# One change to a transformer-block kernel: in the pass over peer_u, 64 of 256 tokens take their rows by indexed gathers

## What is computed

```python
def peer_ffn(h, wq, subkeys, u_tab, v_tab):
    q = (h @ wq).reshape(bsz, s, PEER_HEADS, 2, PEER_KEY_DIM // 2)
    s1 = jnp.einsum('bshd,kd->bshk', q[:, :, :, 0], subkeys[0]).astype(f32)
    s2 = jnp.einsum('bshd,kd->bshk', q[:, :, :, 1], subkeys[1]).astype(f32)
    v1, i1 = lax.top_k(s1, PEER_TOPK)
    v2, i2 = lax.top_k(s2, PEER_TOPK)
...
    best, pos = lax.top_k(cand, PEER_TOPK)
    eidx = jnp.take_along_axis(cidx, pos, axis=-1)
    gate = jax.nn.softmax(best, axis=-1).astype(h.dtype)
...
        act = jax.nn.gelu(jnp.einsum('td,tkd->tk', hx, u_tab[ex]))
        return jnp.einsum('tk,tkd->td', act * gx, v_tab[ex])
```

## Time and profile before

| what | value |
|---|---|
| runs | 3867.51, 3871.76, 3889.56 us |
| the profiled execution | 3888.6 us, span 3886.9 us |
| TensorE (PE) busy | 3543.7 us, 91% |
| VectorE (DVE) busy | 2507.0 us, 64% |
| ScalarE (ACT) busy | 1260.2 us, 32% |
| GpSimd (POOL) busy | 448.8 us, 12% |
| HBM | 753.14 MB read, 50.57 MB written, 207 GB/s |

### The profile page before, as it was taken

The page is one execution under the profiler, slowest core; times in us unless marked ns, Lnnn a source line. Parts: engine busy times, 40 slices in busy tenths (PEclk is TensorE's granted clock), DMA queues, the critical chain, the costliest instruction groups (busy, mean ns, idle before and its releaser), DMA issues. The chain is left out here.

```text
span 3886.9 us, 46926 instructions
## 1 busy us (share of the span) xinstructions
PE 3543.7 (91%) x19227; PEld 2825.6 (73%) x19227; DVE 2507.0 (64%) x3107; ACT 1260.2 (32%) x1433; POOL 448.8 (12%) x451
## 2 busy tenths in 40 slices
PE   7989878999999999999999799997987999899898
PEld 5756557799999999777777587486854766443576
DVE  6855777589777434778788645655446435695564
ACT  3323233334444433444444333223312101100333
POOL 0011110000110000772223000020000211000000
PEclk8888888999999999999999899998998999899899
DMA  9973476265876666999999553305643111553563
GB/s 357 381 237 123 124 279 241 104 218 188 302 263 244 232 227 223 340 357 379 369 365 386 190 185 123 92 6 168 220 167 109 33 44 55 147 152 125 180 237 141
DMA packets 300245, 807.48 MB, mean 208 GB/s; under 512 B 35120, under 2 KB 126356, under 8 KB 256256
## 3 DMA queue, kind: packets, MB, share of 16 engines
q1 hardware_dynamic: 269904, 674.83, 50.5%
q0 software_dynamic: 27664, 123.36, 8.3%
q10 hardware_dynamic: 2464, 6.29, 0.4%
HBM read 753.14 MB, written 50.57 MB: 207 GB/s over the span
## 5 line engine op out<-in xcount | busy, mean ns | idle before, releaser
L2453 DVE TENSOR_TENSOR expert_w_low<-expert_w,expert_w_high 128x2048 fp32r<-128x2048 f32 x256 | 585.7, 2288 | 334.5 <-ACT expert_w_high L2840 333.9
L2840 ACT ACTIVATE expert_w_high<-expert_w 128x2048 fp32r<-128x2048 f32 x256 | 489.5, 1912 | 321.2 <-DMA expert_w<-in_peer_v_dram 242.0
L2759 PE MATMUL bank<-h_high,expert_w_high 128*128 128x256 f32 x2048 | 583.0, 285 | 10.2 <-DVE expert_w_low L2453 9.2
L2760 PE MATMUL bank<-h_low,expert_w_high 128*128 128x256 f32 x2048 | 580.3, 283 | 0.0
L2761 PE MATMUL bank<-h_high,expert_w_low 128*128 128x256 f32 x2048 | 580.3, 283 | 0.0
L289 DVE TENSOR_TENSOR weights_low<-weights,weights_high 128x1024 fp32r<-128x1024 f32 (+4 forms) x288 | 338.2, 1177 | 328.6 <-ACT weights_high L272 325.4
L272 ACT ACTIVATE weights_high<-weights 128x1024 fp32r<-128x1024 f32 (+4 forms) x288 | 293.7, 1021 | 478.5 <-PE bank L317 391.9
L2759 PEld LDWEIGHTS bank<-h_high,expert_w_high 128*128 128x128 f32 x2048 | 393.9, 192 | 11.3 <-DVE expert_w_low L2453 10.0
L2760 PEld LDWEIGHTS bank<-h_low,expert_w_high 128*128 128x128 f32 x2048 | 394.0, 192 | 0.0
L2761 PEld LDWEIGHTS bank<-h_high,expert_w_low 128*128 128x128 f32 x2048 | 393.8, 192 | 0.0
L2817 PE MATMUL bank<-expert_w_high,gated_acts_halves 128*128 128x512 f32 x512 | 203.5, 398 | 27.6 <-DVE expert_w_low L2453 27.5
(11 more groups left out here) (711 smaller groups left out, 6788.7 us busy)
## 6 DMA issues: line engine op xcount, KB each, us to landing
expert_w<-in_peer_u_dram SPq DMA_DIRECT2D x128, 1024.0 KB, 6.0
expert_w<-in_peer_v_dram SPq DMA_DIRECT2D x128, 1024.0 KB, 8.7
weights<-in_ada_w_dram SPq DMA_DIRECT2D x88, 512.0 KB, 9.2
weights<-in_w_out_dram SPq DMA_DIRECT2D x32, 1024.0 KB, 13.7
weights<-in_w_in_dram SPq DMA_DIRECT2D x32, 960.0 KB, 9.6
weights<-in_w_in_dram SPq DMA_DIRECT2D x32, 928.0 KB, 10.0
weights<-in_w_in_dram SPq DMA_DIRECT2D x56, 512.0 KB, 7.0
s_gates_w<-in_w_in_dram SPq DMA_DIRECT2D x56, 512.0 KB, 3.6
```

Of the source, the lines that this page charges most:

```text
L2453: dve.tensor_tensor(wl[:, n % RING, :], w_sb[:, n % RING, :], wh[:, n % RING, :], ALU.subtract).then_inc(wl_ready, 1)
L2759: pe.matmul(o, uh[:, b, k, :], acts.h[:, k, :], start=(k == 0), stop=False)
L2760: pe.matmul(o, uh[:, b, k, :], acts.l[:, k, :], start=False, stop=False)
L2840: act.activation(wh[:, n % RING, :], w_sb[:, n % RING, :], ACT.Copy).then_inc(wh_ready, 1)
```

## The change

The 64 own tokens leave the dense scores. The halves of the tokens' matrix lie side by side, so that one product of 384 columns takes the high weights with both halves of 192 tokens, and one of 192 the low weights with the high half; both sums stand in one PSUM bank (L2817 and L2818 of the changed kernel), VectorE adds them into `act_sb` (`add_halves`, L2534), and ScalarE applies one GELU per four tiles. The own tokens' picks are chosen first (`choose(1)`, then `choose(0)`). Their 64 lists of rows of peer_u are gathered by POOL from a second copy of the table in its plain order, into two slots (L2779), and VectorE multiplies each with the token's row and sums it in one instruction (`dot`, L2511). The own tokens' rows are made at the start: VectorE adds their halves, TensorE turns them, VectorE copies them. `hot1` with its gate is made by ScalarE as Relu(gate - gate x distance), with eight activations of 128 columns per tile. `own_scores` falls away. `TILE_TIME` is 2.6 for 3.2, the ring of `ada_w` 4 for 8. POOL's requests are interleaved by tile.

```diff
-    def __init__(self, m, ctx, name, kt):
-        self.h = m.sb(ctx, name + "_high", [P, kt, T], F32R)
-        self.l = m.sb(ctx, name + "_low", [P, kt, T], F32R)
+    def __init__(self, m, ctx, name, kt, side_by_side=False):
+        if side_by_side:
+            self.at = (m.nc.sbuf_base + 31) // 32 * 32
+            self.both = m.sb(ctx, name + "_halves", [P, kt, 2, T], F32R)
+            self.h, self.l = self.both[:, :, 0, :], self.both[:, :, 1, :]
+        else:
+            self.h = m.sb(ctx, name + "_high", [P, kt, T], F32R)
+            self.l = m.sb(ctx, name + "_low", [P, kt, T], F32R)
...
-    acts_dram = m.dram("expert_acts", [P, EXPERTS_SIDE, T])
+    acts_dram = m.dram("expert_acts", [P, EXPERTS_SIDE, DENSE])
...
-    TILE_TIME = 3.2
+    TILE_TIME = 2.6
     PIECE_GROUPS = (5, 10, 15, 21)
     LISTED = HK * OWN // P
-    BATCH = 8
+    LEAD, LAST_DOT = 4, 118
...
-        mod = ModulationParts(m, io, st, ctx, "mod_last", (5,), piece=512, ring=8, memory=big.take(10 * CHUNK))
+        mod = ModulationParts(m, io, st, ctx, "mod_last", (5,), piece=512, ring=4, memory=big.take(6 * CHUNK))
+        u_slots = [None, big.take(D)]
...
+        halves_at = (nc.sbuf_base + 31) // 32 * 32
         halves = m.sb(ctx, "gated_acts_halves", [P, 2, STEP, 3 * P], F32R)
+        u_slots[0] = nc.alloc_sbuf_tensor_at("own_u_rows", [P, D], F32, offset=halves_at)[:, :]
+        whole_h = nc.alloc_sbuf_tensor_at("own_h_rows", [P, KD, 2, T], F32, offset=acts.at)
+        own_cols = u_slots[0].rearrange("p (k t) -> p k t", k=KD)
+        own_h = whole_h[:, :, :, DENSE:T].rearrange("p k s t -> p (k s) t")
...
+        score_ring = BankRing(m.banks[4:8], m.sem("score_banks_filled"), m.sem("score_banks_emptied"))
+        h_ring = BankRing(m.banks[0:4], m.sem("own_h_banks_filled"), m.sem("own_h_banks_emptied"))
+        gates_ring = BankRing(m.banks[0:2], m.sem("gates_banks_filled"), m.sem("gates_banks_emptied"))
...
+                def own_columns_twice():
+                    h, l = (view(acts.both[:, 0, i, DENSE:DENSE + 1].bitcast(F32), [[2 * T, KD], [0, 2], [1, OWN]]) for i in range(2))
+                    dve.tensor_tensor(own_cols.rearrange("p k (s t) -> p k s t", s=2), h, l, ALU.add).then_inc(own_doubled, 1)
+
+                def own_rows_of_h():
+                    for c in range(4):
+                        bank = h_ring.get(dve)
+                        if c == 0:
+                            dve.wait_ge(h_ring.filled, 4)
+                        h_ring.free(dve.tensor_copy(own_h[:, 8 * c:8 * c + 8, :],
+                                                    bank[:, :].rearrange("p (a b) -> p a b", b=OWN)))
+                    V(dve.engine_nop())
+
+                def dot(i):
+                    dve.wait_ge(u_loaded[i % 2], 16 * (i // 2 + 1))
+                    rows = u_slots[i % 2].rearrange("p (a b) -> p a b", b=OWN)
+                    dve.scalar_tensor_tensor(out=rows, in0=rows, scalar=1.0, in1=own_h, op0=ALU.mult, op1=ALU.mult,
+                                             accum_out=own_acts[:, i:i + 1]).then_inc(u_used, 1)
...
+                def add_halves(n):
+                    g, t = divmod(n, STEP)
+                    if t == 0 and g >= 2:
+                        dve.wait_ge(acts_stored[g % 2], 16 * (g // 2))
+                    bank = score_ring.get(dve)
+                    score_ring.free(dve.tensor_reduce(act_sb[:, g % 2, t, :], view(bank[:, 0:1], [[1, DENSE], [DENSE, 2]]), AX_X, ALU.add))
...
+                def choose_all():
+
+                    yield from choose(1)
+                    list_own()
+                    plan.listed = plan.tile
+                    yield 1.0
+                    yield from choose(0)
...
-                        V(dve.tensor_tensor(hot1[:, b, :, :], view(st.iota_row[:, 0:1], [[0, TOK], [1, P]]),
-                                            spread(i1T[:, tok], P), ALU.is_equal))
-                        V(dve.tensor_tensor(hot1[:, b, :, :], hot1[:, b, :, :], spread(gateT[:, tok], P), ALU.mult))
-                    else:
...
+                        add_halves(n - 2)
+                    if n == 3:
+                        own_rows_of_h()
+                    if plan.listed is not None:
+                        while len(plan.dots) < LISTED * (n - plan.listed - LEAD) / (LAST_DOT - plan.listed - LEAD):
+                            if len(plan.dots) == LISTED:
+                                break
+                            dot(len(plan.dots))
+                            plan.dots.append(n)
+                    plan.adds.append(mod.n_add)
...
-                    done = n - 6
+                    done = n - 7
...
-                def own_scores(half):
-                    every = bass.AP(tensor=acts_dram.tensor, offset=0, ap=[[1, P * EXPERTS_SIDE * T], [1, 1]])
-                    for i in range(half * BATCH // 2, (half + 1) * BATCH // 2):
-                        pool.indirect_dma_start(own_acts[:, i, 0:1], None, every,
-                                                bass.IndirectOffsetOnAxis(ap=listed[:, 1, i:i + 1].bitcast(U32), axis=0))\
-                            .then_inc(own_loaded[i // BATCH], 16)
-
-                pool.wait_ge(turned_picks, 1)
+                def own_u_rows(i):
+                    if i >= 2:
+                        pool.wait_ge(u_used, i - 1)
+                    pool.indirect_dma_start(u_slots[i % 2], None, io["peer_u_rows"],
+                                            bass.IndirectOffsetOnAxis(ap=listed[:, 0, i:i + 1].bitcast(U32), axis=0))\
+                        .then_inc(u_loaded[i % 2], 16)
...
+                asked = tiles_asked = 0
+                for n in range(plan.listed, TILES):
+                    while asked < LISTED and (asked < 2 or plan.dots[asked - 2] <= n):
+                        own_u_rows(asked)
+                        asked += 1
+                    if n >= plan.gates:
+                        if n == plan.gates:
+                            pool.wait_ge(turned_picks, 1)
+                        end = min(mod.tiles, plan.adds[n] + mod.RING)
+                        mod.on_pool(pool, tiles_asked, end)
+                        tiles_asked = end
...
-                own_scores(0)
-                own_scores(1)
...
-                    o = m.to_act.take(pe)[:, 0:T]
+                    o = score_ring.take(pe)
                     for k in range(KD):
-                        pe.matmul(o, uh[:, b, k, :], acts.h[:, k, :], start=(k == 0), stop=False)
-                        pe.matmul(o, uh[:, b, k, :], acts.l[:, k, :], start=False, stop=False)
-                        mm = pe.matmul(o, ul[:, b, k, :], acts.h[:, k, :], start=False, stop=(k == KD - 1))
-                    m.to_act.put(mm)
+                        pe.matmul(o[:, 0:2 * DENSE], uh[:, b, k, :], acts.both[:, k, :, 0:DENSE], start=(k == 0), stop=False)
+                        mm = pe.matmul(o[:, DENSE:2 * DENSE], ul[:, b, k, :], acts.h[:, k, 0:DENSE], start=False, stop=(k == KD - 1))
+                    score_ring.put(mm)
...
+                    if n == 1:
+                        m.to_dve.take_all(pe)
+                        pe.wait_ge(own_doubled, 1)
+                        for c in range(4):
+                            bank = h_ring.take(pe)
+                            for k in range(4 * c, 4 * c + 4):
+                                mm = pe.transpose(bank[:, k % 4 * P:(k % 4 + 1) * P], own_cols[:, k, :], st.ident[:, :])
+                            h_ring.put(mm)
...
+                def gated_onehots(g, half):
+                    b, first = g % 2, half * TOK // 2
+                    if g == 0 and half == 0:
+                        act.wait_ge(turned_picks, 1)
+                    for e in range(first, first + TOK // 2):
+                        t = g * TOK + e
+                        ins = act.activation(hot1[:, b, e, :], st.iota_row[:, 0:P], ACT.Abs, bias=i1T[:, t:t + 1])
+                    ins.then_inc(apart, 1)
+                    act.wait_ge(apart, 2 * g + half + 1)
+                    for e in range(first, first + TOK // 2):
+                        t = g * TOK + e
+                        ins = act.activation(hot1[:, b, e, :], hot1[:, b, e, :], ACT.Relu,
+                                             bias=gateT[:, t:t + 1], scale=minus_gate[:, t:t + 1])
+                    ins.then_inc(hot1_ready, 1)
+
+                def gelu(g):
+                    act.wait_ge(score_ring.emptied, STEP * (g + 1))
+                    act.activation(act_sb[:, g % 2, :, :], act_sb[:, g % 2, :, :], ACT.Gelu_apprx_tanh).then_inc(acts_ready, 1)
+
                 for n in range(TILES):
                     g, t = divmod(n, STEP)
-                    if t == 0 and g >= 2:
-                        act.wait_ge(acts_stored[g % 2], 16 * (g // 2))
-                    bank = m.to_act.get(act)
-                    m.to_act.free(act.activation(act_sb[:, g % 2, t, :], bank[:, 0:T], ACT.Gelu_apprx_tanh))
-                    if t == STEP - 1:
```

(15 more changed lines are left out.)

177 lines of the change are left out of this document (91 added, 86 removed).

## The result

The changed kernel takes **3959.84 us** (median of 4 runs, 3954.8 to 3966.87) against 3877.44 of the kernel before on the same chip: ratio **1.0213** [1.0194, 1.0231]. It is slower by some 82 us; 3848 was forecast, and the range ended at 3935.

The account below looks back on a forecast made before the run. It took TensorE to bound the first pass and the DMA engines the second. Terms +7 +1 -12 -13 -7 summed to -24 us: 3864.6 against the profiled 3888.6, or 3848 against the median; range 3795 to 3935.

Parts of the forecast that it names:

- Tiles 48 to 95 ... I take 318, +1: First pass, tiles making gates: DMA engines would need 318 us where 317 were taken, so 1 us longer.
- Costed at nothing: List of effects priced at zero: SP's later activations store, gated one-hots on ScalarE, the ring of ada_w at four pieces.
- TensorE's pair 0.285 us, with a floor for 192 columns: First-pass products: 0.173 us for 384 columns plus 0.112 for 192, limited by weight load; 4.56 us a tile.
- Reduction 0.55, dot 2.346: VectorE, first pass: 0.55 us per tile to reduce PSUM numbers, 2.346 us for each of 64 dot products.
- One-hots on ScalarE at 0.295: ScalarE, tiles 48 to 95: eight activations of 128 columns per tile at 0.295 us each.
- Tiles 0 to 47, +7: Start of first pass, priced by VectorE's work and its stands: 304 us for 297, 7 us longer.
- Here the gain ends: the DMA engines replace TensorE as the bound: Tiles 48 to 95: DMA engines at 370 to 383 GB/s would bind at the same pace as TensorE did.
- Tiles 96 to 127, -12 and -13: End of first pass: tiles 96 to 117 12 us shorter, tiles 118 to 127 13 us shorter with TensorE binding.
- Second pass, -7: Second pass: 64 small gathers of scores go, 24 tiles at 0.28 us less each, 7 us shorter.
- Gathers late: Rival, tiles 27 to 117: VectorE stands in its queue behind late gathers; 3933 us, slower; chance 0.13.
- 192 columns at the plain rate: Rival: the 192-column product misses the reduced rate, a tile costs 8.1 us, TensorE binds again; 4164 us; chance 0.07.
- SP's later store of activations, covered: SP's store at n - 7 for n - 6 priced at zero, since a group's buffer is used again eight tiles on.

Follow-up runs that it names:

- e3: The kernel before with one edit, the products of the gates and their copy two tiles later: 3948.8 us, ratio 1.0183.
- e9: The changed kernel with a third buffer for hot2 and nothing else: 3890.8 us, ratio 1.0051.
- e10: e9 with ScalarE's copies of the gates ahead of its one-hots and both stores issued by ScalarE: 3850.1 us, ratio 0.9929.
- e13: e8 without the 64 gathers of peer_u and the 64 dots: 3791.7 us, ratio 0.9776.
- e5: e2 with the store of the gates issued by ScalarE instead of SyncE: 3877.2 us, ratio 0.9999.
- e6: e5 with the activations' store also issued by ScalarE: 3873.0 us, ratio 0.9993.
- e2: The changed kernel with hot2 made one tile later and a shift of one tile instead of two: 3889.1 us, ratio 1.0036.
- e11: e8 with both stores back on SyncE: 3869.5 us, ratio 0.9977.
- e8: The changed kernel with hot2 one tile later, both stores issued by ScalarE, and ScalarE's copies of the gates ahead of its one-hots: 3847.7 us, ratio 0.9929.
- e7: e6 without the 64 gathers of peer_u and the 64 dots: 3814.4 us, ratio 0.984.
- e1: The changed kernel with hot2 made in the second tile of a group, nothing else: 3889.0 us, ratio 1.0039.
- e4: The changed kernel without the 64 gathers of peer_u and the 64 dots: 3896.4 us, ratio 1.0055.
- e12: The changed kernel with only ScalarE's copies of the gates ahead of its one-hots: 3896.6 us, ratio 1.0061.

## Why the prediction was wrong

**The step that failed** is "Tiles 48 to 95 ... I take 318, +1": +106.7 was measured. It was priced as the largest of four works, each at its rate: VectorE 286, TensorE 262, ScalarE 273, DMA 318. The works were right (busy 273 and 271 for VectorE and ScalarE), but the sum has no term for the waits between them. The shift in `group_after` is part of the change; the list "Costed at nothing" has SyncE's later store, the one-hots and the ring of `ada_w`, and not the one wait on which the shift bears, `hot_used`. I looked at which engine gets what, not at how many tiles lie between a buffer's copy and its reuse, though `hot2` still had two buffers. The runs showed in its place a serial round of VectorE, TensorE and ScalarE over two tiles, 18.3 us in the trace for 13.2 forecast: it appears with the shift alone (e3, +71) and goes with a third buffer alone (e9, -69). None of the rivals was it either: the slower one put the stand at the dots.

Point by point:
- *TensorE's pair 0.285 us, with a floor for 192 columns*: 0.28, right, at full clock. The step says nothing of the lower clock; 0.54 in a stretch where TensorE idles. In the round above that is 2.8 us more for a tile's scores (7.4 for 4.56); no run here removes it alone, so its share in the 107 us stays open.
- *Reduction 0.55, dot 2.346*: 0.550 and 2.282, right. *One-hots on ScalarE at 0.295*: too low, the two kinds of steps take 0.386 and 0.483, 2.9 us for the eight of a tile where 2.4 were put. In the forecast this costs nothing; in the round it does.
- *Tiles 0 to 47, +7*: -0.3. VectorE is busy for 279.5 us where 287 were put, and idle for about 9.5 where 17 were put; the wait at the turn to the gates did not come.
- *Here the gain ends: the DMA engines replace TensorE as the bound*: not in the changed kernel (share 0.75). e10, without the wait, comes near it: 325.0 us at 365 GB/s and a share of 0.94, against 318 forecast. That fits the forecast bound, hidden under a larger one.
- *Tiles 96 to 127, -12 and -13*: -3.4 and -8.5, -11.9 together. The last ten tiles run 5.06 us apart, not 4.56. ScalarE stood 36.9 us for tiles of peer_u in the 80 us from 1554, at a DMA share of 0.88; without gathers these tiles take 162.8 (e13).
- *Second pass, -7*: -14.0, past even its end with the unpriced reads of activations (-13). One run is a weak measure: with the gathers in place the second pass of the changed kernel and its variants, whose edits put no work into it, takes 591.5 to 602.6 us, and that of the kernel before and its two variants 615.9 to 618.9. The gain is 13 to 27 us, some 20 in the mean, so the term was too small. No run says why.
- *Gathers late* (second rival): 7.8 us of waits in 64; refuted. *192 columns at the plain rate* (third rival): a pair takes 0.28 us; refuted.
- *SP's later store of activations, covered*: nothing speaks against it. SyncE's waits in the stretch have no row for that store, and moving it gave 4 us, inside the interval (e5 to e6). What the list does not name is the store of the gates, which the same shift also moves: SyncE waits 39.4 us for it in the changed kernel and 69.1 in e2. Moving that one gives 12 us (e2 to e5), and both stores together 22 where the copies come first (e11 to e8). That hot2's wait hid this one is part of why the first repairs stopped near 3889.

That e8 lands on 3847.7, the number forecast, is luck and no support: it is another kernel, its stretch is 16 us over, and its second pass takes 591.5 us where the forecast has some 610. Against the kernel before, its profile has +15.0 in the stretch, -14.2 in tiles 96 to 127 and -25.2 in the second pass. The time that TensorE was freed of in the first pass is for the most part not gained: tiles 0 to 47, where VectorE is full, stay at 289, and the stretch gets longer.

## What to carry to other kernels

When a change moves a consumer of a buffer by k steps, count for each buffer how many steps lie between the release and the reuse. Here three tiles left 0 to 9 us of wait (before, e2, e5, e6, e7, e9), two left 36 to 81 (e1, e8, e11, e13) and one left 69 to 207 (after, e3, e4, e12). What falls to one or two is to be priced as a serial round through all the engines in it; that a sum of busy times shows room for every engine says nothing on this. When the bound is taken away from an engine that was always busy, list every stand which it covered (here SyncE's for the gates, 73 us at no cost before; the two stores off SyncE are worth 22 us in the repaired version). And take away one wait at a time with the time of the next in view: three different repairs of the first wait all stopped at 3889 to 3897 us.

## What was not expected of the hardware

TensorE's clock fell to the 1.2 GHz level in a stretch where the engine idled again and again for only a few us (4.49 before 1190.56, 8.1 at most before a product), and rose within a tile's products, at 1196; the mean was 0.84 over 425 us. A pair of products took 0.54 us instead of 0.28, and that sat inside the round of waits, which it made longer. Whether the longer round then makes TensorE idle and slow down more is not shown: no run holds the clock. The kernel before was busy there for 318.96 of 320 us and had 1.00.

The floor by the weight load is not seen in each product. By starts, the pair of 0.28 us splits into 0.20 from the wide product to the narrow one and 0.08 from that to the next wide one; only the sum of the two is what 0.173 + 0.112 gave. The Trainium skill, "TensorE: Matmul & The Clock Gate", section "LDWEIGHTS", has 107 ns for a load of 128 columns; the 0.08 is below it and the pair's mean of 0.14 above it. So as a floor for every single product it is not borne out by these starts; that the prediction's sum for the pair came out right does not show that its split did.
